# First expert pair fed by a one-hot product, in a two-layer decoder trunk with a mixture of experts

## Chip, cores and metric

The kernel runs on one core of one Trainium2 chip. The metric is the device time of one execution in microseconds (us), as the median of several runs. All times below are of the kernel before the change.

## What is computed

512 tokens of width 1024 pass through two layers. Each layer adds a token mixer and then a mixture of 32 experts. All arithmetic is float32. Cut to what matters here:

```
for i in range(2):
    mk, mv = memory_kv(mem, mem_norm[i], w_mem_kv[i])          # 256 memory tokens
    hn = rms_norm(x, norm_mix[i])
    x  = x + mixer_i(hn, mk, mv) @ w_out[i]                    # layer 0: RG-LRU; layer 1: sparse attention
    h  = rms_norm(x, norm_ffn[i])
    # group of 8 experts (top 1 of 4), then the top 2 experts in that group, for each token
    y  = sum over the token's two experts e of  gate * (silu(h @ w_gate[e]) * (h @ w_up[e])) @ w_down[e]
    x  = x + y
```

## The kernel before

**The experts.** They are worked off in 16 pairs per layer, each pair as one tile of 128 rows: up to 64 tokens of the even expert and up to 64 of the odd one. What goes beyond 64 is left to a loop at the layer's end. A pair needs six weight tiles ("units") of 2 MB each: gate of both experts (j = 0, 1), up (2, 3), down (4, 5). The units go into a ring of 10 places in the arena. SP issues all their loads in order (`weights`, L525 to L536, through `pair_weights`). The first 10 are issued on events of the stage before; each later one waits until TensorE is done with the place's former unit (`gate_psum`, `up_psum`, `y_psum`).

**One pair on TensorE** (`pair`, L1517): gate product (L1480, 32 instructions, written x32), combination of the pair before with x (L1502), up product (L1480), the rest of that combination, transposes of the hidden rows (L1486), then the transposes of the *next* pair's tokens (`tokens_T`, L1473), and the down product (L1494). A float32 product shows two instructions for each matmul in the program. VectorE scales the transposed tokens by norm_ffn into tokT (`tokens_out`, L2063).

**Tokens of a pair.** The normalised rows are stored in DRAM (scratch_xn, L619). GpSimd gathers the 128 rows of a pair with an indirect DMA (`gather`, L723 to L734) into xg; TensorE transposes them. The first pair's gather, transposes and scaling stand before the first pair, the second's inside it, and so on, so there are 17 gathers per layer.

**The handover from mixer to experts.** TensorE follows an order written out by hand: the out products, the transposes of x (fT), router products (route) for four tiles of tokens; then `rank` (how many tokens before this one chose the expert, L1444 to L1452), then `table` (L1456 to L1462), which turns ranks into a table of token numbers for each pair. VectorE picks the experts between route and rank (L1950 to L1984), computes the mixing weights (L1988 to L2001), then the places (L2008 to L2017) and, behind the table, tabP, from which the gathers take their indices. In layer 0, the four memory products of layer 1 (memK.0, memK.1, memV.0, memV.1; L1155) stand between: one before rank, one between rank and table, two behind the table. SP waits for memV.1 before it loads the second pair's up units.

**PSUM banks** are handed out round robin over a list of jobs (`plan`, L148): a job's bank is its number mod 8 and it waits until the job 8 before has been read out by ScalarE or VectorE.

**The start.** ScalarE issues the loads of mem_norm, norm_mix and norm_ffn into `gains` (L792), in runs of 8 numbers; VectorE waits for all three before it spreads the gain over the first transposed tile (L1629, two instructions of 128x512 for each of four tiles of tokens). The first mixer product (xs.0) waits for the eighth of them and for its weights, loaded in two halves (L555).

**Middle of layer 0's mixer.** On TensorE: ..., xs.5, xq.0, xq.1, the six block gates, two norm sums, the transposes of the memory rows (memT, 16), then the memory products, which wait until VectorE has spread two gains over each of four banks (L1629, eight instructions). On VectorE, these stand behind `log_decays(1)` (L1707 to L1716), which waits for the block gates. The first attention logits (x_logits, L1282) wait for the normalised memory keys, the last of VectorE's chain there: two reciprocals of 128x512 (L1623), three scans (L1731), a third reciprocal.

## Time and profile before

| what | us |
|---|---|
| median of 3 runs | 1498.46 (1496.92 to 1500.74) |
| the profiled execution's own time | 1493.24 |
| its span, first to last instruction | 1491.4 |
| TensorE busy | 1385.7 (93%) |
| VectorE busy | 590.6 (40%) |
| ScalarE busy | 326.6 (22%) |
| TensorE's mean granted clock | 0.976 of full |
| main queue (q1, all loads of SP) | 447.96 MB, 72.8% of the 16 DMA engines' time |

The span is one profiled execution; the runs are others of the same program. "Busy" of TensorE counts matmuls up to their modelled ends. A granted clock of 1.00 is 2.4 GHz, 0.50 is 1.2 GHz. Layer 0's experts run from about 266 to 726 us, layer 1's from about 1022 to 1484 us.

### The profile page before, as it was taken

Reading aid. Unit: us, or ns where it says so; the run is one execution under the profiler, and the core shown is the slowest. Engines: PE = TensorE matmul, PEld = TensorE weight load, DVE = VectorE, ACT = ScalarE, POOL = GpSimd, SP = SyncE. Lnnn points to the kernel's source line nnn. Section 1 sums busy time; section 2 is a strip of 40 time slices with the busy share of each in tenths; the row PEclk is TensorE's granted clock in tenths of the full one; section 3 lists DMA queues with packets and bytes.
Section 4 is the critical chain, followed back from the end, with each engine's and each line's share of the span. In section 5 each row is a group of like instructions: output and inputs, shape, how many; then the busy total and the mean of one; then the engine's idle time right before and its main releaser. Section 6 shows DMA issues by size and latency. Waiting matters only on the chain.

```text
span 1491.4 us, 16620 instructions
## 1 busy us (share of the span) xinstructions
PE 1385.7 (93%) x6272; PEld 618.7 (41%) x6337; DVE 590.6 (40%) x1084; ACT 326.6 (22%) x632; POOL 103.0 (7%) x199
## 2 busy tenths in 40 slices
PE   7989998999999999999899978976999999999987
PEld 3445456333333334333454555442333333333333
DVE  5555124133333334233649774132334334332334
ACT  4445111101101101111337664110111111110110
POOL 1001000200000000000000132003000000000000
PEclk9999999999999999999999999987999999999999
DMA  9105365999999999999800020737999999999994
GB/s 315 68 0 198 129 263 203 357 428 426 428 426 425 427 428 428 427 427 419 296 0 1 25 93 1 309 152 275 425 428 427 426 427 426 427 427 427 429 426 203
DMA packets 57332, 457.53 MB, mean 307 GB/s; under 512 B 15516, under 2 KB 22220, under 8 KB 32312
## 3 DMA queue, kind: packets, MB, share of 16 engines
q1 hardware_dynamic: 50928, 447.96, 72.8%
q0 software_dynamic: 5504, 8.68, 1.6%
q8 instruction: 42, 0.69, 0.2%
q10 hardware_dynamic: 840, 0.06, 0.0%
q14 instruction: 18, 0.15, 0.0%
HBM read 459.50 MB, written 10.53 MB: 315 GB/s over the span
## 4 chain that ended last, share of the span: by engine, by line
PE 63%; DMA 23%; DVE 8%; ACT 3%; issue 1%; POOL 0%; SPq 0%; ACTq 0%; DVEq 0%; POOLq 0%
PE ps L1480 20%; PE ps L1155 19%; DMA arena<-in_moe_w_up 14%; PE ps L1494 10%; DMA arena<-in_moe_w_gate 9%; PE ps L1502 6%; PE ps L1473 1%; DVE mix L1774 1%; ACT arena L999 1%; DVE small L1773 1%; DVE arena L1850 1%; DMA mix<-scratch_xn,whole 1%; PE ps L1486 1%; DVE xT L1629 1%; DMA gains<-in_norm_ffn 1%
## 5 line engine op out<-in xcount | busy, mean ns | idle before, releaser
L1480 PE MATMUL ps<-arena,xT 128*64 128x512 f32 x2048 | 461.9, 605 | 26.0 <-DMA arena<-in_moe_w_gate 20.5
L1480 PEld LDWEIGHTS ps<-arena,xT 128*64 128x64 f32 x2048 | 151.6, 139 | 319.2 <-issue 319.2
L2086 DVE TENSOR_TENSOR x<-ps,x 128x1024 f32<-128x1024 f32 x120 | 146.5, 1225 | 219.0 <-PE ps L1502 216.7
L1494 PE MATMUL ps<-arena,xT 128*64 128x512 f32 x1024 | 226.8, 595 | 0.0
L1155 PE MATMUL ps<-xT,arena 128*128 128x512 f32 x384 | 170.6, 599 | 1.8 <-DVE xT L1629 1.4
L1502 PE MATMUL ps<-mix,xT 128*128 128x512 bf16 x660 | 157.4, 379 | 6.4 <-issue 4.8
L1494 PEld LDWEIGHTS ps<-arena,xT 128*64 128x64 f32 x1024 | 70.7, 137 | 131.8 <-issue 127.9
L1155 PE MATMUL ps<-arena,mix 128*128 128x512 f32 (+1 forms) x288 | 119.4, 570 | 0.0
L1502 PEld LDWEIGHTS ps<-mix,xT 128*128 128x128 bf16 x720 | 65.5, 98 | 119.5 <-issue 48.7
L1155 PEld LDWEIGHTS ps<-xT,arena 128*128 128x128 f32 x384 | 72.6, 192 | 92.5 <-issue 89.6
L2069 DVE SCALAR_TENSOR_TENSOR xT<-ps,cur,xT 128x512 f32<-128x512 f32 x32 | 24.0, 751 | 207.3 <-PE ps L1480 207.3
L2079 DVE TENSOR_TENSOR mix<-ps,mix 128x512 f32<-128x512 f32 x60 | 41.5, 692 | 158.4 <-ACT mix L1101 158.4
L1095 ACT ACTIVATE xT<-ps 128x512 f32<-128x512 f32 x32 | 19.1, 597 | 387.1 <-PE ps L1486 387.1
L1101 ACT ACTIVATE mix<-ps 128x512 bf16<-128x512 f32 x60 | 35.8, 597 | 201.9 <-PE ps L1494 201.9
L1155 PEld LDWEIGHTS ps<-arena,mix 128*128 128x128 f32 x288 | 53.8, 190 | 56.7 <-issue 55.8
L728 POOL CAST whole<-tabP 128x1 int32 (+1 forms) x34 | 6.3, 184 | 968.3 <-PE ps L1473 779.7
L1091 ACT ACTIVATE xT<-ps 128x512 f32<-128x512 f32 x32 | 19.1, 597 | 219.0 <-PE ps L1480 219.0
L721 POOL TENSOR_SCALAR arena<-arena,small 128x256 f32<-128x256 f32 (+3 forms) x80 | 39.3, 510 | 248.6 <-DVE small L1789 189.7
L2063 DVE TENSOR_TENSOR xT<-ps,gains 128x512 f32<-128x512 f32 x68 | 43.8, 687 | 22.7 <-PE ps L1473 18.4
L1473 PE MATMUL ps<-ident,mix 128*128 128x128 f32 x272 | 37.0, 280 | 12.9 <-DMA mix<-scratch_xn,whole 12.2
L1936 DVE TENSOR_TENSOR x<-ps,x 128x512 f32<-128x512 f32 x16 | 11.1, 692 | 90.3 <-PE ps L1155 90.3
L2082 DVE TENSOR_TENSOR mix<-mix 128x512 bf16<-128x512 f32 x60 | 41.2, 687 | 2.9
(268 smaller groups left out, 1110.8 us busy)
## 6 DMA issues: line engine op xcount, KB each, us to landing
arena<-in_moe_w_gate SPq DMA_DIRECT2D x64, 2048.0 KB, 32.3
arena<-in_moe_w_up SPq DMA_DIRECT2D x64, 2048.0 KB, 32.0
arena<-in_moe_w_down SPq DMA_DIRECT2D x64, 2048.0 KB, 34.9
arena<-in_w_out SPq DMA_DIRECT2D x2, 4096.0 KB, 13.5
arena<-in_dsa_w_in SPq DMA_DIRECT2D x1, 5120.0 KB, 16.1
arena<-in_w_mem_kv SPq DMA_DIRECT2D x2, 2048.0 KB, 9.0
scratch_xn<-arena SPq DMA_DIRECT2D x8, 512.0 KB, 2.9
scratch_rep<-scratch_bias SPq DMA_DIRECT2D x1, 3840.0 KB, 17.9
```

Source lines behind the costliest of these rows:

```text
L721: ins = pool.tensor_scalar(buf[:, h, 0:width], buf[:, h, 0:width], inv[:, h:h + 1], 1.0, ALU.mult, ALU.mult)
L1101: act.activation(y_hi[part, c, :], ps[part, BANK_Y + c, :], ACT.Copy).then_inc(q["y_high"], 1)
L1155: ins = pe.matmul(b[part, cols], l, r, start=i == 0, stop=i == len(pairs) - 1)
L1473: ins = pe.transpose(ps[:, BANK_XT[k // 4], (k % 4) * P:(k % 4) * P + n], xg[0:n, k::KD][:, 0:P], ident[0:n, 0:n])
L1480: ins = pe.matmul(ps[e * CAP:(e + 1) * CAP, bank, :], tokT[:, k, e * CAP:(e + 1) * CAP], rows_in[u][:, k, :], start=k == 0, stop=k == KD - 1)
L1494: ins = pe.matmul(ps[e * CAP:(e + 1) * CAP, BANK_Y + c, :], hT[:, j, e * CAP:(e + 1) * CAP], rows_down[u][:, j, c * 512:(c + 1) * 512], st ...
L1502: ins = pe.matmul(ps[:, 4 + 2 * (t % 2) + c, :], onehot[part, t * P:(t + 1) * P], y[part, c, :], start=q == 0, stop=q == 2)
L2063: dve.tensor_tensor(tokT[:, 4 * q:4 * q + 4, :], ps[:, BANK_XT[q], :].rearrange("p (k n) -> p k n", k=4), gains[:, 3 * L + 2, 4 * q:4 * q ...
L2069: dve.scalar_tensor_tensor(out=h_sb[part, :], in0=ps[part, BANK_UP, :], scalar=c[part, 1:2], in1=silu[part, :], op0=ALU.mult, op1=ALU.mult ...
L2079: dve.tensor_tensor(y_rest[part, c, :], ps[part, BANK_Y + c, :], y_hi[part, c, :], ALU.subtract).then_inc(q["y_rest"], 1)
L2082: dve.tensor_tensor(y_lo[part, c, :], y_rest[part, c, :], y_mi[part, c, :], ALU.subtract).then_inc(q["y_low"], 1)
L2086: dve.tensor_tensor(x[:, t, :], ps[:, b:b + 2, :].rearrange("p a n -> p (a n)"), x[:, t, :], ALU.add).then_inc(s_, 1)
```

## The change

1. **First pair's tokens.** Gather 0, its transposes and its scaling are gone in both layers. After rank, VectorE makes first_hot, a 0/1 matrix that says which token stands at which place of experts 0 and 1; TensorE multiplies the normalised rows (xn_ffn, still in SBUF) by it: 32 matmuls of 128x128, two banks. The features then stand in blocks of 128 (k·128 + p, not p·8 + k), so the first pair's gate and up weights are loaded in that order, and norm_ffn is needed in that order too: it is loaded into prm_rows by one more DMA, transposed with the parameters and copied over the mem_norm part of gains.
2. **Order of the handover.** Layer 0: all four memory products stand before rank. Both layers: rank, first.0, first.1, table. SP issues the first pair's sixth unit (it lies over xn_ffn) behind first.1. TensorE waits for the old banks behind the first gate product.
3. **Layer 1's units.** The second pair's up units are issued right behind the first five units.
4. **Start.** norm_mix is loaded first and waited for alone; the last half tile is scaled by ScalarE (four instructions of 128x128); xs weights come in three thirds.
5. **Middle of the mixer.** memT is transposed between xq.0 and xq.1; VectorE spreads it before log_decays(1).

```diff
@@ mixer_steps
-             ("xq", 0), ("xq", 1), ("gates", 1), ("sq.xq", 0), ("sq.xq", 1), ("memT", 0), ("mem", 0), ("sq.memK", 0),
+             ("xq", 0), ("memT", 0), ("xq", 1), ("gates", 1), ("sq.xq", 0), ("sq.xq", 1), ("mem", 0), ("sq.memK", 0),
@@ SP
+                if kind < 2 and by_block:
+                    sp.dma_start(rows_in[u], src.rearrange("(k p) n -> p k n", p=P)).then_inc(done, 16)
...
-                weights(L, p * 2 + j % 2, j // 2, u, landed[u])
+                weights(L, p * 2 + j % 2, j // 2, u, landed[u], isinstance(p, int) and p == 0)
...
-                    for h in range(2):
-                        c0 = h * LRU // 2
+                    for h in range(3):
+                        c0 = h * LRU // 3
...
+                    sp.dma_start(prm_rows[R_FFN:NROW, :], a["norm_ffn"].rearrange("l (k p) -> (l k) p", p=P)).then_inc(ld["prm"], 16)
...
                 for j in range(5):
                     pair_weights(L, j, j, 0, NP * L, True)
+                if L:
+                    for j in (2, 3):
+                        pair_weights(L, j, 6 + j, 1, NP * L + 1, True)
...
                 sp.wait_ge(xn_stored, 16 * NT * (L + 1))
-                pair_weights(L, 5, 5, 0, NP * L, True)
                 if L == 0:
                     wait_filled(sp, "1.memV.1")
-                for j in (2, 3):
-                    pair_weights(L, j, 6 + j, 1, NP * L + 1, True)
+                    for j in (2, 3):
+                        pair_weights(L, j, 6 + j, 1, NP * L + 1, True)
+                wait_filled(sp, f"{L}.first.1")
+                pair_weights(L, 5, 5, 0, NP * L, True)
@@ GpSimd
-                gather(L, 0, N, True)
-                gather(L, 1, N + 1)
+                gather(L, 1, N + 1, True)
@@ ScalarE
-            for n, name in enumerate(("mem_norm", "norm_mix", "norm_ffn")):
+            for n, name in ((1, "norm_mix"), (0, "mem_norm"), (2, "norm_ffn")):
...
+                    name = f"0.xT.{NT - 1}.1"
+                    act.wait_ge(ld["gmix"], 16)
+                    wait_filled(act, name)
+                    for k in range(4):
+                        ins = act.activation(xT[:, 4 + k, (NT - 1) * P:S], bank(name)[:, k * P:(k + 1) * P], ACT.Copy,
+                                             scale=gains[:, 1, 4 + k:5 + k])
@@ TensorE
                 if L == 0:
-                    memory_product(1, 0)
+                    for i in range(4):
+                        memory_product(1, i)
                 b = open_bank(f"{L}.rank")
...
+                pe.wait_ge(first_placed, L + 1)
+                for h in range(2):
+                    b = open_bank(f"{L}.first.{h}")
+                    for k in range(4):
+                        for t in range(NT):
+                            ins = pe.matmul(b[:, k * P:(k + 1) * P], xn_ffn[:, t, (4 * h + k) * P:(4 * h + k + 1) * P],
+                                            first_hot[:, t].rearrange("p e n -> p (e n)"), start=t == 0, stop=t == NT - 1)
+                    ins.then_inc(filled, 1)
                 b = open_bank(f"{L}.table")
...
-                    pe.wait_ge(m["xt_sbuf"], n * 2 + (2 * L + 2))
+                    if first:
+                        wait_emptied(pe, f"{L}.first.1")
+                    else:
+                        pe.wait_ge(m["xt_sbuf"], n * 2)
                     both(BANK_GATE, units[0:2], m["gate_psum"])
...
-                pe.wait_ge(gathered, 16 * ((NP + 1) * L + 1))
-                tokens_T(m["xt_psum"])
@@ VectorE
                     x_rows(0)
-                    dve.wait_ge(ld["gains"], 48)
-                    for t in range(1, NT):
+                    x_rows(1)
+                    dve.wait_ge(ld["gmix"], 16)
+                    x_spread(0)
+                    for t in range(2, NT):
...
-                    log_decays(1)
...
+                    line.link(dve.tensor_copy(gains[:, 0:6:3, :], prm[:, R_FFN:NROW].rearrange("p (l k) -> p l k", l=2)))
+                    log_decays(1)
...
                 dve.tensor_tensor(choice[:], oh[0], oh[1], ALU.add).then_inc(chosen, 1)
+                wait_filled(dve, f"{L}.rank")
+                line.link(dve.scalar_tensor_tensor(out=first_row, in0=ranks[:, :, 0:2], scalar=1.0, in1=choice[:, :, 0:2],
+                                                   op0=ALU.add, op1=ALU.mult))
+                dve.tensor_tensor(first_hot, iota_tok[:, 1:CAP + 1].unsqueeze(1).unsqueeze(1).to_broadcast([P, NT, 2, CAP]),
+                                  first_row.unsqueeze(3).to_broadcast([P, NT, 2, CAP]), ALU.is_equal).then_inc(first_placed, 1)
...
                 dve.tensor_copy(dest[:], row).then_inc(routed, 1)
+                for h in range(2):
+                    spread_gain(f"{L}.first.{h}", tokT[:, 4 * h:4 * h + 4, :], 3 * L, h, P)
```

## Rows read from the trace of the kernel before

**Rows 1.** The page, 40 equal slices of 37.3 us: what the DMA engines moved
```profile
GB/s 315 68 0 198 129 263 203 357 428 426 428 426 425 427 428 428 427 427 419 296 0 1 25 93 1 309 152 275 425 428 427 426 427 426 427 427 427 429 426 203
```

**Rows 2.** The chain that ended last, whole program: start, us, what
```profile
309.97 7.02 PE ps L1494 x32
...
337.63 7.02 PE ps L1494 x32
...
651.93 42.62 DMA arena<-in_moe_w_gate
...
1408.25 41.92 DMA arena<-in_moe_w_gate
```

**Rows 3.** Timeline of SP's queue, both handovers: start, us, engine, line, what
```profile
262.43 0.80 SPq L532 DMA_DIRECT2D arena<-in_moe_w_up  x2
272.86 0.80 SPq L535 DMA_DIRECT2D arena<-in_moe_w_down  x2
...
932.57 0.83 SPq L532 DMA_DIRECT2D arena<-in_moe_w_gate  x2
...
1032.13 0.80 SPq L535 DMA_DIRECT2D arena<-in_moe_w_down  x2
```

**Rows 4.** Table of stretches, both handovers: busy us (count) of PE, PEld, DVE, ACT, POOL; PEclk, DMA share, GB/s
```profile
275.00:277.50 2.50, 2.50 (x14) 1.01 (x12) 0.00 (x0) 0.00 (x0) 1.35 (x2) 1.00 1.37 230
...
1025.00:1028.00 3.00, 3.00 (x9) 0.86 (x8) 0.00 (x0) 0.00 (x0) 0.99 (x1) 0.52 0.05 15
1028.00:1032.10 4.10, 4.10 (x22) 1.55 (x20) 0.00 (x0) 0.00 (x0) 2.91 (x4) 1.00 0.02 1
1032.10:1035.00 2.90, 2.90 (x16) 1.01 (x14) 0.00 (x0) 0.60 (x1) 2.29 (x3) 1.00 0.76 91
```

**Rows 5.** Timeline of PE, handover of layer 1: start, us, engine, line, what
```profile
998.40 0.27 PE L1451 MATMUL ps<-choice,ones_b 128*128 128x32 bf16 x4
1002.84 3.65 PE L1460 MATMUL ps<-xT 128*128 128x64 f32 x16 [4.17 <-DVE xT L2020]
1018.71 1.95 PE L1473 MATMUL ps<-ident,mix 128*128 128x128 f32 x8 [12.22 <-DMA mix<-scratch_xn,whole]
1022.19 16.77 PE L1480 MATMUL ps<-arena,xT 128*64 128x512 f32 x64 [1.54 <-DVE xT L2063]
```

**Rows 6.** Timeline of PE, handover of layer 0
```profile
241.16 3.70 PE L1155 MATMUL ps<-arena 128*128 128x256 f32 x16
...
265.74 13.95 PE L1480 MATMUL ps<-arena,xT 128*64 128x512 f32 x64 [1.54 <-DVE xT L2063]
```

**Rows 7.** The chain, layer 1's mixer (64 instructions, 132 columns)
```profile
762.46 7.20 PE ps L1244 x64
```

**Rows 8.** A group of VectorE by form: busy us, mean ns
```profile
L2014 DVE TENSOR_TENSOR xT<-iota_tok,small 128x256 f32<-128x256 f32 x8 | 3.4, 425 | 0.3
```

**Rows 9.** The chain, start of the program
```profile
1.73 8.06 DMA gains<-in_norm_ffn
10.85 1.29 DVE xT L1629 x2
...
17.76 8.71 PE ps L1155 x16
```

**Rows 10.** Timeline of PE, its first transposes
```profile
7.25 1.94 PE L1164 MATMUL ps<-ident,mix 128*128 128x128 f32 x8 [7.25 <-DVE mix L1613]
```

**Rows 11.** Timeline of PE, middle of layer 0's mixer
```profile
102.75 8.86 PE L1155 MATMUL ps<-mix,arena 128*128 128x256 f32 x32 [4.39 <-DVE mix L1629]
111.45 7.07 PE L1155 MATMUL ps<-arena,mix 128*128 128x256 f32 x32
...
126.17 2.00 PE L1282 MATMUL ps<-arena 64*128 64x256 f32 x16
```

**Rows 12.** Timeline of VectorE, the same stretch
```profile
116.92 1.22 DVE L1731 TENSOR_TENSOR_SCAN arena<-arena 128x512 f32<-128x512 f32 x1
120.13 3.35 DVE L1623 RECIPROCAL mix<-mix 128x512 f32<-128x512 f32 x1 [1.99 <-ACT mix L831]
```

More of the change, by code:

```diff
@@ L142, in pt_reader, with x_reader @@
     return "act" if (s + g) % 2 else "dve"
+def x_reader(L, t, h):
+    return "act" if (L, t, h) == (0, NT - 1, 1) else "dve"
 def plan():
@@ L256, in plan @@
             j.add(memory_products(1)[0], "act")
+        if L == 0:
+            for name in memory_products(1)[1:]:
+                j.add(name, "act")
         j.add(f"{L}.rank", "dve")
-        if L == 0:
-            j.add(memory_products(1)[1], "act")
+        for h in range(2):
+            j.add(f"{L}.first.{h}", "dve")
         j.add(f"{L}.table", "dve")
-        if L == 0:
-            for i in (2, 3):
-                j.add(memory_products(1)[i], "act")
     return j
@@ L399, in hybrid_trunk @@
         route_area = flatT[:, 2816:4096]
-        place_hot = flatT[:, 512:1536].rearrange("p (k t c n) -> p k t c n", k=2, t=NT, c=2)
-        expert_pay = flatT[:, 1536:2048].rearrange("p (k t c e) -> p k t c e", k=2, t=NT, c=2)
+        place_hot = flatT[:, 1024:2048].rearrange("p (k t c n) -> p k t c n", k=2, t=NT, c=2)
+        first_hot = flatT[:, 2048:2560].rearrange("p (t e n) -> p t e n", t=NT, e=2)
+        expert_pay = flatM[:, 1024:1536].rearrange("p (k t c e) -> p k t c e", k=2, t=NT, c=2)
+        first_row = small[:, 24:24 + 2 * NT].rearrange("p (t e) -> p t e", t=NT)
         pay_t = small[:, 64:80].rearrange("p (k t c) -> p k t c", k=2, t=NT)
@@ L406, in hybrid_trunk @@
         i8 = route_area[:, 1248:1280].bitcast(U32).rearrange("p (t n) -> p t n", t=NT)
-        ld = {n: sem(f"ld_{n}") for n in ["mem", "x0", "x1", "x2", "x3", "win0", "win1", "prm", "onehot", "gains", "broute", "wkv", "win", "winq", "wing", "wv", "wg",
+        ld = {n: sem(f"ld_{n}") for n in ["mem", "x0", "x1", "x2", "x3", "win0", "win1", "win2", "prm", "onehot", "gmix", "gains", "broute", "wkv", "win", "winq", "wing", "wv", "wg",
                                           "wout", "wr", "bias", "wuv", "ovl"]}
@@ L519, in last_bank @@
             return (jobs.number[f"1.xT.{t}.0"] + c) % 8
-        assert sorted(last_bank(t, c) for t in range(NT) for c in range(2)) == list(range(8)) and last_bank(2, 1) == BANK_Y + 1
+        assert sorted(last_bank(t, c) for t in range(NT) for c in range(2)) == list(range(8))
+        assert all(last_bank(t, c) % 2 == c for t in range(NT) for c in range(2)) and BANK_Y % 2 == 0
         block = ctx.enter_context(nc.Block())
@@ L527, in _, with weights @@
         def _(sp):
-            def weights(L, e, kind, u, done):
-                if kind < 2:
+            def weights(L, e, kind, u, done, by_block=False):
+                if kind < 2 and by_block:
+                    src = a["moe_w_gate" if kind == 0 else "moe_w_up"][L, e]
+                    sp.dma_start(rows_in[u], src.rearrange("(k p) n -> p k n", p=P)).then_inc(done, 16)
+                elif kind < 2:
                     src = a["moe_w_gate" if kind == 0 else "moe_w_up"][L, bass.ds(e, 1)]
@@ L1462, in _, with banks_emptied @@
                 ins.then_inc(filled, 1)
-                if L == 0:
-                    memory_product(1, 2)
-                    memory_product(1, 3)
                 for n in range(state["n"] - 8, state["n"]):
-                    who = jobs.reader[n]
-                    pe.wait_ge(emptied[who], jobs.before[n][who])
+                    if n % 8 == BANK_GATE:
+                        pe.wait_ge(emptied[jobs.reader[n]], jobs.before[n][jobs.reader[n]])
+                def banks_emptied():
+                    for who in ("act", "dve"):
+                        pe.wait_ge(emptied[who], jobs.before[state["n"] - 1][who])
                 def tokens_T(s_, n=P):
@@ L1651, in _ @@
                     rows_normalise(L, "mem", range(2), lambda t: mem[:, t, :], lambda t: mem[:, t, :])
+                    dve.wait_ge(ld["gains"], 32)
                 else:
@@ L2001, in _ @@
                                                 pay_t[:, k].unsqueeze(3).to_broadcast([P, NT, 2, NE]), ALU.mult))
-                wait_filled(dve, f"{L}.rank")
-                ranks = bank(f"{L}.rank")[:, 0:NT * NE].rearrange("p (t e) -> p t e", t=NT)
                 place = [small[:, 16 + NT * k:16 + NT * (k + 1)] for k in range(2)]
```

52 lines of the change are left out of this document (32 added, 20 removed).

## The prediction

> **What bounds the kernel now.** I read the page's slices first. In the middle of either layer's experts the DMA engines move 425 to 429 GB/s [rows 1], one slice like the next. TensorE is busy nearly all the time there too, so the chain of waits has to say who paces whom. It does so late in each layer: the last pair's gate weights are issued at 651.93 and 1408.25 us and land 42.62 and 41.92 us later, at 694.55 and 1450.17, and the chain runs through these landings [rows 2]. Early in a layer it runs through TensorE alone, with a period of 337.63 − 309.97 = 27.66 us a pair [rows 2]. Fifteen periods, 414.9 us, from the first gate product of layer 0 at 265.74 [rows 6] come to 680.6; the weights come at 694.55. So the loads are the bound, by 14 us. In layer 1 the same sum, from 1022.19 [rows 5] with 2.8 us for a gate product of 16.77 instead of 13.95 us [rows 5, 6], gives 1439.9 against 1450.17: 10 us.
>
> What starts that stream of loads? SP's timeline shows it: ten units fit into the ring, and the eleventh is issued at 272.86 in layer 0 and at 1032.13 in layer 1 [rows 3], when the first gate product is done. In layer 1 the DMA engines have nothing to do before that moment (share 0.02 to 0.05) [rows 4]. From that issue to the last gate landing pass 694.55 − 272.86 = 421.7 us and 1450.17 − 1032.13 = 418.0 us. **A microsecond by which the first gate product ends sooner is a microsecond off the layer**, as long as the stretch behind it keeps its length; and whatever TensorE gains in the mixer of layer 0 moves that product. Behind the last landing the work is unchanged.
>
> **Start.** VectorE waits for norm_ffn's landing at 1.73 + 8.06 = 9.79 us, the first two spreads start at 10.85, a tile's scaling later, and xs.0 starts at 17.76 [rows 9]. With norm_mix issued first and alone, the first spreads can follow the first transposes, which end at 7.25 + 1.94 = 9.19 [rows 10]; allowing 0.45 us for the tile scaled in between, that is 1.2 us sooner. VectorE then has the same sequence, one spread of 1.29 / 2 = 0.65 us [rows 9] shorter, since ScalarE takes it. Its transposed bank is there a spread earlier, so its four small copies end about when VectorE does. 1.2 + 0.65 = 1.9 us saved. Bounds: 0.6 (only the spread moves off) and 2.5. The new load of norm_ffn rows adds one issue on SP ahead of mem and of everything behind it, under half a microsecond on a queue whose loads are wanted tens of microseconds later; a smaller first third can't be later than the first half was. Cost nothing; if it is not covered, at most 1 us at the parameters.
>
> **Middle of the mixer.** TensorE idles 4.39 us before the memory products and then takes 8.86 us for 32 instructions whose twins take 7.07 [rows 11]: a half-speed clock after the idle time, 1.8 us. Both go: memT's spreads now lie under xq.1 (7 us against 8 spreads of 0.65 = 5.2). TensorE would win 6.2 us. What is late next is VectorE: its last scan ends at 118.14 and its third reciprocal waits 1.99 us more for ScalarE [rows 12]. Its chain before that doesn't get shorter, because the gates themselves come 1.9 us later (memT stands before them now) while the 5.2 us of spreads leave the path behind them and ScalarE's roots take most of their place. The normalised memory keys then come at 118.14 + 3.35 + 0.65 = about 122.1, instead of 120.13 + 3.35 + 0.65 = 124.1, and x_logits, now behind gate.0 at 126.17 [rows 11], begins then. Saved 4.1 us, with 1.4 us of new idle time. Bounds: 2.0 and 6.2. I take 4.1. The start and this give **6.0 us** on everything in layer 0 behind.
>
> **Handover in layer 0.** Before: 241.16 to 265.74, 24.6 us from the first memory product to the first gate product [rows 6]. After, on TensorE: four memory products at 7.07 for two [rows 11], 14.1; rank with its hand-over 0.5; VectorE's first_row (an estimate of 0.3, hand-over in it) and first_hot. The latter is twice the 128x256 of L2014 at 425 ns [rows 8], less its fixed part: 0.7. Then 32 matmuls of 128x128. The nearest row is layer 1's 64 instructions of 132 columns in 7.20 us [rows 7]: 7.2. The table has 16 instructions, 3.65 us at half clock [rows 5], so 1.9 at full. Two hand-overs, 0.2. Sum 14.1 + 0.5 + 1.0 + 7.2 + 1.9 + 0.2 = 24.9. **0.3 us later, no gain**: gather 0 was hidden under the memory products, which now cover nothing. VectorE's work between rank and table, 4.2 us [rows 5], now stands behind first_hot, under the 7.2 us; if it doesn't, the table waits. Bounds: 1 sooner and 2.5 later.
>
> Behind the first gate product the queue is emptier than it was: up units of the second pair went out at 262.43 [rows 3] and were still under way at 272.86, with a gather and the eight scatters (a stretch at 230 GB/s with a share of 1.37 [rows 4] shows what scatters do). Now they go out about 7 us sooner relative to TensorE. The difference of 421.7 and 418.0 is what that costs; I give back half: **−1.8 us**, bounds 0 and −3.7.
>
> **Handover in layer 1.** Before: rank is done at 998.40 + 0.27 = 998.7, table 1002.84, 12.22 us of waiting for the gather, transposes 1018.71, scaling, then gate and up product together from 1022.19 [rows 5], the gate half's event at 1032.1 [rows 3]. After: first_hot done at 999.8. TensorE has had little to do for some microseconds, so it starts at half clock. How long? Before, work began at 1022.19, the clock still stood at 0.52 until 1028 and at 1.00 after it [rows 4]: 5.6 us. The first 5.6 us of the product do 25 instructions at 0.225 us, the other 39 take 4.4: done at 1009.8. Table 1.9, gate from 1011.7, first half until 1018.7 at full clock. 1032.1 − 1018.7 = 13.4 us sooner. The scatters, which before fell mostly on an idle queue (91 GB/s at the end of them [rows 4]), now fall on the stream: +1.2. **Layer 1 gains 12.2 us.** Bounds: all at half clock, 64 at 0.225 = 14.4, table 3.65, half a cold gate product, gives 1.1 + 14.4 + 3.7 + 7 + 2.8 behind 998.7, that is 1027.7: a gain of 4.4, less 1.2. All at full clock: 15.
>
> A rule bears on this. The rows show an idle TensorE at half clock and a return some microseconds into the work. The Trainium skill, "TensorE: Matmul & The Clock Gate", Part 1, says that the point of the return varies between runs of the same kernel. By it, the 1.1 us hole before first.0 in layer 0 may or may not cost a half-speed spell; priced by the 8.86 against 7.07 us [rows 11], the sum would be 1.8 us more with one.
>
> The block-ordered weights of the first pair come in runs of 2 KB instead of 16. They are issued from 932.57 [rows 3], 75 us before they are wanted at about 1010; I cost them at nothing. Layer 1's second up units, moved ahead, are 2 of 10 units loaded before the stream anyway and no longer press on the gap; nothing waited for them. The 17th gather was 0.5 MB in each layer outside the stream: nothing.
>
> **Sum**, against the profiled execution: 1493.24 − 6.0 + 0.3 − 1.8 − 12.2 = 1473.5. The median of the runs lies 5.2 us above that execution (1498.46), so I forecast **1479 us** (1478.7). A measurement of this kernel can tell some 0.3%, 4.5 us, from no change.
>
> **Rivals.**
> - *Cold product* (0.12). The clock stays at half through first.0 and first.1 in layer 1 and falls in layer 0's hole as well. For it: the clock was still at 0.52 up to 1028 [rows 4], with a table and transposes done in between. Against: neither of those was a long piece of work. Gain 3.2 in layer 1 instead of 12.2, 1.8 lost in layer 0: 1478.7 + 9.0 + 1.8 = 1489.5.
> - *VectorE holds the mixer, or the stream doesn't follow* (0.12). The mixer gives only its lower bounds (2.6 instead of 6.0) and the stretch of 418 to 422 us grows by 2 because scatters, gather and loads meet: 1484.
> - *The change does nothing that counts* (0.03): the first gate product is not what releases the stream, but a later event such as the first down product, itself unmoved. Against: the eleventh unit goes out 7.12 us behind the start of the gate product in layer 0, 272.86 against 265.74 [rows 3, 6], which is one gate product. 1494 to 1499.
> - *Slower: the block-ordered units arrive late* (0.02). Four units, 8.4 MB, in 2 KB runs, between 932.57 [rows 3] and first.1 at about 1010. They decide only if they take longer than 77 − 15 = 62 us, that is below 135 GB/s, and to turn 20 us of gain into a loss of 5 they would need 87 us, 96 GB/s. None of the full slices goes so low [rows 1]. That would be 1504. The Trainium skill, "DMA: Bandwidth & Descriptors", "Why small descriptors are slow", has a fixed overhead per packet that speaks against shorter runs; by its figures (3 cycles on 64) the four units would take 1 us more, an estimate, and all of it would be hidden.
>
> The forecast itself has 0.71. **Range**: its own terms run from 1473 (mixer 8.7, stretch −3.7, layer 1 at 14) to 1486; the low end with some run-to-run spread 1472, the high end takes in most of the cold product, 1489. Faster by over 0.3%: 0.94 (all but the last two and a few unlucky sums); within 0.3%: 0.04; slower: 0.02.
>
> **What would show it.** xs.0 near 15.9; x_logits 0 some 6 us sooner than 126.17; first gate product of layer 0 near 260.0, so layer 0's eleventh unit near 267; last gate landing near 687; between rank and the first gate product of layer 1 13 us instead of 23.5, with no wait on a gather; the clock at 1.00 in that gate product. A wait of TensorE on VectorE before the table, or on a unit of the first pair, would prove me wrong, as would an eleventh unit that goes out sooner without the last landing following it.

## The result, and the profile after

| | before | after |
|---|---|---|
| median, us | 1498.24 (4 runs, 1496.92 to 1500.74) | 1473.82 (4 runs, 1472.13 to 1474.37) |
| profiled execution, us | 1493.24 | 1473.94 |
| its span, mean granted clock | 1491.4, 0.976 | 1472.0, 0.986 |

The ratio is 0.9833, with a 95% interval of 0.9816 to 0.985: 24.4 us faster by the medians, 19.3 by the two profiled executions. The forecast was 1479, and 19.7 us between the profiles. One execution of experiment 10 took 3039.51 us, about twice as long as all others, for a reason that no trace shows; it is left out of that experiment's median.

The page of the changed kernel, the 40 slices of what the DMA engines moved:

```profile
GB/s 292 96 0 226 139 247 195 385 427 426 427 427 427 426 427 428 427 427 427 321 2 1 1 119 2 310 199 297 427 427 425 427 427 426 427 427 428 428 426 199
```

The plateau is as high as before [rows 1]; it only starts sooner. The start and the middle of the mixer, on TensorE (start, us, engine, line, what, and in brackets the idle time before it):

```profile
15.49 7.10 PE L1181 MATMUL ps<-xT,arena 128*128 128x512 f32 x16 [1.34 <-DVE xT L1668]
...
94.05 7.07 PE L1181 MATMUL ps<-mix,arena 128*128 128x256 f32 x32
...
117.76 2.67 PE L1309 MATMUL ps<-arena 64*128 64x256 f32 x16 [2.00 <-DVE arena L1663]
120.36 8.11 PE L1181 MATMUL ps<-xT,arena 128*128 128x512 f32 x16
```

xs.0 starts 2.3 us sooner than in [rows 9] and takes 7.10 instead of 8.71 us. The 4.39 us before the memory products [rows 11] are gone. The logits start 8.4 us sooner and now wait 2.00 us for VectorE; behind that wait they and the next gate product take 2.67 and 8.11 us where 2.00 [rows 11] and 7.13, as the later gate products of this profile, are usual: in this profile part of the gain is paid back in clock (a "spell" below is such a stretch at a granted clock of one half). The first out product starts at 166.6 instead of 173.4.

The two handovers on TensorE; first layer 0's:

```profile
230.64 1.16 PE L1190 MATMUL ps<-ident,x 128*128 128x128 f32 x8 [0.78 <-DVE x L1983]
232.62 1.95 PE L1181 MATMUL ps<-w_route,xT 128*128 128x36 f32 x16 [0.83 <-ACT xT L1099]
234.40 15.75 PE L1181 MATMUL ps<-arena 128*128 128x256 f32 x64
...
251.52 7.38 PE L1488 MATMUL ps<-xT,arena 128*128 128x128 f32 x64 [1.03 <-issue]
258.74 1.90 PE L1495 MATMUL ps<-mix,xT 128*128 128x64 f32 x16
```

then layer 1's, where [rows 5] had a wait of 12.22 us and a first gate and up product that began at half clock (16.77 us, now 13.96):

```profile
992.18 0.18 PE L1476 MATMUL ps<-choice,before 128*128 128x32 bf16 x1 [4.80 <-DVE choice L2031]
...
993.75 10.16 PE L1488 MATMUL ps<-xT,arena 128*128 128x128 f32 x64 [1.03 <-issue]
1003.75 1.90 PE L1495 MATMUL ps<-mix,xT 128*128 128x64 f32 x16
1005.57 13.96 PE L1516 MATMUL ps<-arena,xT 128*64 128x512 f32 x64
```

The stream behind them. SP's queue issues the eleventh unit at

```profile
267.69 0.82 SPq L548 DMA_DIRECT2D arena<-in_moe_w_down  x2
...
1012.70 0.80 SPq L548 DMA_DIRECT2D arena<-in_moe_w_down  x2
```

and the last gate weights come, by layer 0's timeline of TensorE and by layer 1's chain of waits, at

```profile
687.52 7.09 PE L1516 MATMUL ps<-arena,xT 128*64 128x512 f32 x32 [1.51 <-DMA arena<-in_moe_w_gate]
```

```profile
1390.60 40.15 DMA arena<-in_moe_w_gate
```

From the issue to this: 419.8 us in layer 0 (about 419.6 to the landing itself), and 1390.60 + 40.15 − 1012.70 = 418.05 us in layer 1, against 421.7 and 418.0 from issue to landing before. Both layers still end behind a landing of gate weights; all of the gain but the 2 us of layer 0's stretch lies ahead of the stream.

### The profile page after: what moved, and what is told of

Its sections match the earlier page's. It is cut to its first block and busy times, and to the rows that moved or that the text cites. A ratio compares the mean times of both kernels' runs of the same rounds, so it can differ in the third digit from the quotient of the medians.

```text
span 1472.0 us, 16830 instructions
## 1 busy us (share of the span) xinstructions
PE 1389.9 (94%) x6384; PEld 628.3 (43%) x6449; DVE 592.4 (40%) x1088; ACT 326.9 (22%) x636; POOL 101.0 (7%) x195
## 5 line engine op out<-in xcount | busy, mean ns | idle before, releaser
L1130 ACT ACTIVATE mix<-mix 128x512 bf16<-128x512 f32 x60 | 37.6, 627 | 7.2 <-DVE mix L2133 7.2
```

Source lines behind the costliest of these rows:

```text
L1130: act.activation(y_mi[part, c, :], y_rest[part, c, :], ACT.Copy).then_inc(q["y_mid"], 1)
```

## Experiments

Twelve experiments, in three groups; each group shares its chip and its runs of the kernel before, whose medians were 1497.09 (18 runs), 1496.73 (17) and 1497.77 (11). The theory under test is the prediction's: TensorE's own path to the first gate product sets the stream's start, and the stream then has a fixed length. The changed kernel itself ran only beside the result's four runs of before, so its 1473.82 comes from another group than the medians set against it. Three experiments that moved nothing measurable (6, 8 and 11, one in each group) came to 1473.42, 1473.47 and 1473.34, which supports that comparison; the ratio to each group's own runs of before is given as well.

**1. The kernel before, once more** (label before_again, no edit).

> The kernel before, once more, with a profile. The change moved the median by 24.4 us and the profiled execution by 19.3 (1493.24 to 1473.94). Theory: the mechanisms give 19.3, and the other 5 are the spread of the kernel before, whose runs lie 1493 to 1501. Then its profile shows, in some stretch (a clock or a landing), what is longer in an ordinary run than in the one first profiled. Rival: the first profile was of an ordinary run and another chip gives 1498 with the same stretches all a little longer.

Measured 1497.23 (10 runs, 1495.54 to 1499.38), ratio 1.0009 (0.9998 to 1.0019). Its profiled execution, 1497.96 us, is 4.7 longer than the one that the prediction rests on. Its TensorE shows where:

```profile
242.36 6.06 PE L1155 MATMUL ps<-arena 128*128 128x256 f32 x16
...
255.34 1.97 PE L1460 MATMUL ps<-xT 128*128 128x64 f32 x16 [3.03 <-DVE xT L2020]
...
269.39 13.96 PE L1480 MATMUL ps<-arena,xT 128*64 128x512 f32 x64 [1.54 <-DVE xT L2063]
...
744.79 9.11 PE L1203 MATMUL ps<-xT,arena 128*64 128x512 f32 x32
```

The first memory product takes 3.70 us in [rows 6] and 6.06 here. The handover of layer 0 (first memory product to first gate product) takes 27.0 us here, 24.6 in [rows 6], and 26.7 and 27.6 in experiments 2 and 3, which have it unchanged; layer 1's first projection 9.11 us, against 7.09 in the first profile and 8.81 and 9.24 in 2 and 3. The first profile was the lucky one in both places.

**2. The new start alone, on the kernel before** (start_only).

```diff
-            for n, name in enumerate(("mem_norm", "norm_mix", "norm_ffn")):
+            for n, name in ((1, "norm_mix"), (0, "mem_norm"), (2, "norm_ffn")):
...
-                    dve.wait_ge(ld["gains"], 48)
+                    dve.wait_ge(ld["gmix"], 16)
```

> The kernel before with the new start alone (norm_mix first, last half tile on ScalarE, xs weights in thirds). Theory: xs.0 at 15.5 instead of 17.8, and at full clock, 7.1 instead of 8.7 us; together 2.3 to 3.9 us sooner at the second product. Later in the mixer the memory products wait for VectorE, which also starts sooner, so all of it reaches x_logits and the end: 1493.2 to 1495 against 1497.1. Rival (the middle waits for VectorE's gates, which do not move with the start): under 1 us.

Measured 1494.44 (12 runs), ratio 0.9979 (0.9968 to 0.999): 2.3 us by medians, 3.1 by the ratio. xs.0 starts at 15.4 but takes 8.80 us, so the clock's part did not come in this profile. The lead of the start is kept up to the router:

```profile
171.13 20.87 PE L1168 MATMUL ps<-arena,mix 128*128 128x512 f32 x48
...
237.11 3.19 PE L1168 MATMUL ps<-w_route,xT 128*128 128x36 f32 x16 [0.83 <-ACT xT L1086]
```

The first out product starts 2.3 us sooner than in the first profile and 2.5 sooner than in experiment 1 (173.41 and 173.63), router product 3 also 2.3 and 2.5 sooner (239.39 and 239.60). The first gate product, at 266.80, is 2.6 us sooner than in experiment 1, but 1.1 later than in the first profile with its short handover.

**3. New start and new middle, on the kernel before** (mixer_only).

```diff
-             ("xq", 0), ("xq", 1), ("gates", 1), ("sq.xq", 0), ("sq.xq", 1), ("memT", 0), ("mem", 0), ("sq.memK", 0),
+             ("xq", 0), ("memT", 0), ("xq", 1), ("gates", 1), ("sq.xq", 0), ("sq.xq", 1), ("mem", 0), ("sq.memK", 0),
```

> The kernel before with only the new start and the new middle of layer 0's mixer. Theory: all of layer 0 behind it moves by 6.8 us, as the two profiles show at the first out product, the eleventh unit's issue and the last gate landing follow one for one, layer 1 follows: 6 to 8 us below the kernel before. Rival (the loads would have come when they come anyway): less than 2 us.

Measured 1488.39 (9 runs), ratio 0.9945 (0.9932 to 0.9958): 8.7 us. The mixer's part of the change is about a third of the whole. Less experiment 2, it gives the middle 6.4 us by the medians and 5.1 by the ratios. The profiles of 2 and 3, both with 8.80 us for xs.0, say 4.3: the first out product starts at 166.85 instead of 171.13. The logits wait as in the changed kernel, but no spell follows:

```profile
119.61 2.00 PE L1296 MATMUL ps<-arena 64*128 64x256 f32 x16 [2.00 <-DVE arena L1638]
121.54 7.13 PE L1168 MATMUL ps<-xT,arena 128*128 128x512 f32 x16
```

**4. The changed kernel with its old middle** (middle_undone). The order of the steps goes back too.

```diff
+                    log_decays(1)
                     for mt in range(2):
...
                     line.link(dve.tensor_copy(gains[:, 0:6:3, :], prm[:, R_FFN:NROW].rearrange("p (l k) -> p l k", l=2)))
-                    log_decays(1)
```

> The changed kernel with the middle of layer 0's mixer as it was: memT transposed behind the norm sums, VectorE's log_decays(1) ahead of its spreads. Theory (the middle gained 4.1 us by the prediction, about 4.5 by the landmarks of the before-and-after traces, and all of it reaches the end): 1477.5 to 1478.5 us, the 4.4 us wait before the memory products back, first attention logits 4 to 5 us later than 117.8. Rival (the gain of the middle came from the start, by banks and clock, and the move itself is worth little): 1475 or less.

Measured 1476.35 (4 runs, 1474.99 to 1478.44), ratio 0.9865: 2.5 us slower than the changed kernel by medians, 4.8 by the two ratios, whose groups of before runs differ by 1.5 us. By the medians the theory's size fell short, and the rival's 1475 was passed. The logits are 4.3 us late, as expected, but the first out product only 2.7 (169.35 against 166.64), because the changed kernel's profile has a spell behind the logits and this one has none. That spell is not the rule: of the eight profiles with the 2.00 us wait, only the changed kernel's and experiment 5's have it. Against experiment 6, whose mixer is the changed kernel's and whose profile has neither this spell nor one in xs.0, the middle is worth 4.3 us again, as between 2 and 3. First out products of this experiment and of 6:

```profile
169.35 20.87 PE L1181 MATMUL ps<-arena,mix 128*128 128x512 f32 x48
```

```profile
165.01 20.87 PE L1178 MATMUL ps<-arena,mix 128*128 128x512 f32 x48
```

This profile also shows the four memory products without a spell, behind the same two holes (idle times of 0.79 and 0.83 us) that the changed kernel has:

```profile
237.11 14.06 PE L1181 MATMUL ps<-arena 128*128 128x256 f32 x64
```

**5. The one-hot product done twice** (first_twice).

```diff
+                        for t in range(NT):
+                            pe.matmul(b[:, k * P:(k + 1) * P], xn_ffn[:, t, (4 * h + k) * P:(4 * h + k + 1) * P],
+                                      first_hot[:, t].rearrange("p e n -> p (e n)"), start=t == 0, stop=t == NT - 1)
+                    for k in range(4):
```

> The changed kernel with the one-hot product done twice in both layers (same result, 64 instructions more in each). Theory: 7.0 us more before the first gate product in each layer, and the whole stream of loads moves by that: 14 us slower than the changed kernel. Rival: the loads pace the layer and TensorE has 10 to 14 us in hand in each, so the extra product vanishes in it: 0 to 3 us.

Measured 1487.40 (4 runs), ratio 0.9941 (0.9919 to 0.9962): 13.6 us slower than the changed kernel by medians, 15.0 by the profiled executions, 16 by the two ratios. The added halves on TensorE in layer 0, and the end of the stream in layer 1's chain:

```profile
251.90 3.81 PE L1488 MATMUL ps<-xT,arena 128*128 128x128 f32 x32 [1.03 <-issue]
...
262.69 3.74 PE L1492 MATMUL ps<-xT,arena 128*128 128x128 f32 x32
```

```profile
1404.31 41.65 DMA arena<-in_moe_w_gate
```

Its eleventh unit of layer 1 goes out at 1027.96 and the last gate weights land 418.0 us later, at 1445.96. The product and its copy take 14.36 us in layer 0 (266.26 − 251.90, the table's start) against 7.22, and 16.15 against 10.00 in layer 1, where the cold part is a little shorter: 13.3 us more on TensorE. In the profiles the eleventh unit of layer 1 goes out 15.3 us later and the last weights land 15.2 later, so the stream follows its event one for one; the 2 us beyond the added work gathered on the way (0.4 by the first out product, 1 in layer 0's stretch, the rest in layer 1's mixer). The rival's 0 to 3 us is out: what is added ahead of the stream comes out in full, in both layers.

**6. Layer 1's up units not moved ahead** (up_not_early).

```diff
-                if L:
-                    for j in (2, 3):
-                        pair_weights(L, j, 6 + j, 1, NP * L + 1, True)
```

> The changed kernel with layer 1's units in the old order (second pair's up units behind the stores of the rows). Theory: they then load in the time between the last store and the first gate product in which the queue has nothing to do, and nothing waits for them: 0 us, within 1 of the changed kernel. Rival (the new order is worth something): the sixth unit or the first gather lands so late behind them that the first down product or the second pair's tokens wait: 2 to 5 us more.

Measured 1473.42 (4 runs), ratio 0.985 (0.9828 to 0.9871): nothing that these runs can tell, as argued. In its profile layer 1's eleventh unit goes out 1.3 us sooner than the changed kernel's (1011.43), by luck of the clock in layer 0, and the last weights land only 0.2 sooner (1430.57): a stretch of 419.1 us, where the changed kernel and experiments 5, 7, 9, 10, 11 and 12 have 417.1 to 418.4. So that part of the change may be worth about 1 us; one profile doesn't show it.

**7. The first pair's weights in long runs** (long_runs).

```diff
-                weights(L, p * 2 + j % 2, j // 2, u, landed[u], isinstance(p, int) and p == 0)
+                weights(L, p * 2 + j % 2, j // 2, u, landed[u], False)
```

> The changed kernel with the first pair's gate and up weights of both layers loaded in the old order of rows (16 KB in one piece for each partition instead of eight of 2 KB). The features no longer match the weights of that pair, so its part of the output is of mixed-up features; the work is otherwise the same. Theory (the pieces of 2 KB cost issue time on SP and nothing on the path, because these units are wanted 75 us later): time within 0.5 us of the changed kernel; issue of two such units on SP falls from 10 us to 1 us or less. Rival (the small pieces hold the stream or other loads beside them): 1 us or more less.

This kernel leaves out the matching order of features and weights, so its output is not the program's. Measured 1475.38 (4 runs, 1472.82 to 1475.88), ratio 0.9855 (0.9834 to 0.9875): not faster. The median is 1.6 us above the changed kernel's where 0.5 was allowed for, and the two sets of runs overlap; in the profiles the last weights land 1.0 us sooner. SP's queue with block order and with long runs, first pair of layer 1:

```profile
927.02 10.32 SPq L542 DMA_DIRECT2D arena<-in_moe_w_up  x2
```

```profile
927.08 1.12 SPq L545 DMA_DIRECT2D arena<-in_moe_w_up  x2
```

and what the DMA engines did (stretch, busy us and count of PE, PEld, DVE, ACT, POOL, granted clock, DMA share, GB/s), again the changed kernel first:

```profile
930.00:945.00 15.00, 15.00 (x42) 7.16 (x41) 2.99 (x5) 3.21 (x5) 0.00 (x0) 1.00 1.04 386
```

```profile
930.00:945.00 15.00, 15.00 (x43) 7.11 (x42) 2.99 (x5) 3.21 (x5) 0.00 (x0) 1.00 1.00 428
```

Runs of 2 KB cost 10% of the rate in this stretch and hold SP's queue for 5 us a unit, both long before anyone waits.

**8. Rank between the memory products** (rank_second): layer 0's memV.0 and memV.1 stand behind rank.

```diff
-                    for i in range(4):
+                    for i in range(2):
                         memory_product(1, i)
...
+                    for i in range(2, 4):
+                        memory_product(1, i)
```

> The changed kernel with one order undone in part: in layer 0, rank stands between memK.1 and memV.0 instead of behind memV.1. Theory (the stream follows the first gate product 1:1, and what TensorE waits for VectorE's first_row and first_hot is on that path): memV.0 and memV.1 cover the 1.03 us wait before first.0, and the half-clock spell that the trace of the changed kernel shows in this handover has one hole less to begin in. First gate product of layer 0 1.0 to 1.5 us sooner after rank's own place is allowed for (26.2 us from the first memory product becomes about 25), last landing of layer 0 the same amount sooner, time 1.0 to 1.5 us less. Rival (the half-clock spell comes anyway, or another wait takes the hole's place, such as ScalarE's emptying of the banks): within 0.5 us of the changed kernel.

Measured 1473.47 (5 runs), ratio 0.984 (0.9823 to 0.9858): no gain. The wait before the one-hot product is gone, but the handover is as long as it was, 26.1 us:

```profile
235.01 9.97 PE L1182 MATMUL ps<-arena 128*128 128x256 f32 x32
...
245.18 7.15 PE L1182 MATMUL ps<-arena 128*128 128x256 f32 x32
252.17 7.31 PE L1492 MATMUL ps<-xT,arena 128*128 128x128 f32 x64
```

The rival held: 9.97 us for 32 instructions that take 7.07 at full clock. The hole before the one-hot product is gone and the spell came all the same, ahead of it; that leaves the two holes before the memory products as its suspects.

**9. Memory products in the two holes before them** (holes_filled). The order of the last tile in layer 0 becomes out, memK.0, fT.3, memK.1, route.3, memV.0, memV.1, rank.

```diff
+    if L == 0:
+        order = out_order()
+        order.insert(order.index(("fT", 3)), ("mem", 0))
+        order.insert(order.index(("route", 3)), ("mem", 1))
+        return order
```

> The changed kernel with two of layer 0's four memory products moved forward into the two holes of the last tile: memK.0 before the transposes fT.3, memK.1 before route.3; memV.0 and memV.1 stay before rank. Theory (TensorE's own path sets layer 0's first gate product, and the half-clock spell in the memory products follows the two short holes of 0.78 and 0.83 us before it): both holes gone, 1.6 us, and with them the spell of 1.65 us; first gate product of layer 0 at 257.3 to 259 instead of 260.6, time 1.6 to 3.3 us less. Rival 1 (the spell comes elsewhere, as it did in the run with rank second): 0 to 1 us less. Rival 2 (the choice of experts, which now starts 5.5 us later on VectorE, ends behind the memory products): rank waits, nothing gained or a loss.

Measured 1471.04 (5 runs), ratio 0.9819 (0.9802 to 0.9836): 2.8 us less than the changed kernel by medians, 2.1 by the ratios, whose intervals overlap, and 2.3 less than experiment 11 of the same group.

```profile
229.66 3.62 PE L1188 MATMUL ps<-arena 128*128 128x256 f32 x16
233.12 1.04 PE L1197 MATMUL ps<-ident,x 128*128 128x128 f32 x8
234.00 3.62 PE L1188 MATMUL ps<-arena 128*128 128x256 f32 x16
237.45 1.87 PE L1188 MATMUL ps<-w_route,xT 128*128 128x36 f32 x16
239.16 7.15 PE L1188 MATMUL ps<-arena 128*128 128x256 f32 x32
...
256.73 5.80 PE L1525 MATMUL ps<-arena,xT 128*64 128x512 f32 x26
```

No hole, no spell; the first gate product starts 3.8 us sooner (256.73 against 260.57) from the same first out product at 166.6. VectorE's choice of experts stayed under the memory products: rank waits for nothing. How much of the 3.8 us is the edit's stays open: 1.6 us are the holes, but the spell was missing in experiment 4's profile too, with the holes there. Nor did all of it arrive: the last gate product of layer 0 starts 2.0 us sooner (685.56), 421.7 us behind the eleventh unit's issue instead of 419.8, and the profiled execution is 1.4 us shorter.

**10. A gate product before the logits** (gate_ahead).

```diff
-             ("gate", 0), ("x_logits", 0), ("x_logits", 1), ("gate", 1), ("x_turn", 0), ("x_logits", 2),
+             ("gate", 0), ("gate", 1), ("x_logits", 0), ("x_logits", 1), ("gate", 2), ("x_turn", 0), ("x_logits", 2),
```

> The changed kernel with gate.1 of layer 0's mixer ahead of the first attention logits, and each later gate one place earlier. Theory (the 2.00 us in which the logits wait for VectorE's chain, and the half-clock spell behind it, 0.67 + 1.0 us, are the middle's unfinished gain): first out product 2.0 to 3.7 us sooner, time 2 to 3.7 us less. Rival (the wait comes back at the end of the mixer, where the last turn now has one gate product less to cover ScalarE's and VectorE's softmax): less than 1 us.

Measured 1471.24 (5 runs, 1467.99 to 1473.85), ratio 0.9822 (0.9803 to 0.9841): 2.6 us less by medians, 1.6 by the ratios, whose intervals overlap. The wait is gone. The first out product starts at 162.83, 3.8 us sooner than in the changed kernel's profile, but 2.2 sooner than in experiment 6's, which has the wait and no spell: the edit is worth the wait. The first gate product is 2.2 us sooner than the changed kernel's (258.41), since the memory products now take 16.7 us, with a longer spell.

**11. Work for an idle TensorE** (keep_warm): five matmuls between route.3 and rank in layer 1, which rank overwrites.

```diff
+                if L:
+                    pe.wait_ge(rows_normed, rows[L, "ffn", NT - 2])
+                    for i in range(5):
+                        pe.matmul(b[:, 0:256], xn_ffn[:, 0, 0:P], xn_ffn[:, 1, 0:256], start=True, stop=True)
```

> The changed kernel with five matmuls of 128x256 between route.3 and rank in layer 1, while TensorE waits 4.8 us for the choice of experts; what they compute is overwritten by rank and read by nobody. Theory (the one-hot product of layer 1 takes 10.16 us instead of 7.3 because TensorE stood idle before it): 7.3 to 8.5 us for it, time 1.5 to 3 us less. Rival 1 (the two holes that are left, about 0.4 before rank and 1.0 behind it, keep the clock at half all the same): 10.2 us, no change. Rival 2 (at half clock the five take 4.4 us and end behind the choice): up to 0.5 us more.

Measured 1473.34 (5 runs), ratio 0.9832 (0.9812 to 0.9851): nothing to be told from the changed kernel. The table of stretches, the product, and the same product in experiments 7 and 9, without the five matmuls:

```profile
987.00:990.00 3.00, 2.68 (x14) 2.07 (x13) 2.38 (x17) 0.73 (x2) 0.00 (x0) 1.00 0.85 262
990.00:992.00 2.00, 0.00 (x0) 0.00 (x0) 1.86 (x15) 0.80 (x2) 0.00 (x0) 0.96 0.82 319
992.00:994.00 2.00, 0.82 (x15) 0.75 (x16) 1.25 (x6) 0.69 (x1) 0.00 (x0) 0.50 0.98 418
994.00:998.00 4.00, 4.00 (x20) 4.00 (x20) 3.69 (x15) 0.00 (x0) 0.00 (x0) 0.50 1.01 434
```

```profile
993.73 9.74 PE L1492 MATMUL ps<-xT,arena 128*128 128x128 f32 x64 [1.03 <-issue]
```

```profile
993.61 8.89 PE L1488 MATMUL ps<-xT,arena 128*128 128x128 f32 x64 [1.03 <-issue]
```

```profile
992.66 10.33 PE L1497 MATMUL ps<-xT,arena 128*128 128x128 f32 x64 [1.03 <-issue]
```

At full clock the five took 2.40 us and ended at 989.7; TensorE then stood idle until rank, the granted clock fell from 1.00 to 0.50 meanwhile, and the product took 9.74 us. That is no gain: without the five it takes 10.16 us in the changed kernel and 8.89 to 10.33 in experiments 4, 6, 7, 8, 9 and 10. Rival 1 held, with a gap before rank of 2.4 us rather than 0.4, since the five ran at full clock.

**12. Experiments 9, 10 and 11 together** (all_three).

> The changed kernel with all three edits: memory products in the holes, gate.1 ahead of the logits, five matmuls before rank in layer 1. Theory: the three lie one behind another on the path and add, 1473.6 less 5 to 10 = 1464 to 1469 us, faster than both kernels. Rival (half-clock spells removed in one place come back in another, as the run with rank second and the undone middle hint): the sum of the three single gains falls short by 2 us or more.

Measured 1466.51 (5 runs, 1466.26 to 1469.12), ratio 0.9799 (0.9782 to 0.9815): 7.3 us less than the changed kernel by medians, 5.1 by the ratios, where the single gains sum to 5.8 and 3.9. The theory's 1464 to 1469 us held and the sum did not fall short. It is the fastest of all the kernels here, and its interval lies clear of the changed kernel's. Here the five matmuls ran at half clock (4.09 us) and left a gap of 0.78 us before rank; the one-hot product took 9.01 us, within the spread above. Its eleventh unit of layer 1 goes out at 1005.52 and its last gate weights land at

```profile
1383.38 40.05 DMA arena<-in_moe_w_gate
```

which is 1423.43, again 417.9 us later.

## Why the prediction was right, point by point

- **The bound and the 1:1 rule** held. The event, that is the issue of the eleventh unit, moved by 5.2 us in layer 0 (272.86 to 267.69) and 19.4 in layer 1 (1032.13 to 1012.70), the last landings by 7.3 (of which 2 are a shorter stretch) and 19.4, the end by 19.3. Experiments 5 and 12 moved the event in both directions with stretches of 418.0 and 417.9. That is layer 1, where all but two profiles (4 and 8, whose chains don't pass that landing) show 417.1 to 419.1. In layer 0 the stretch is less fixed, as the point on the emptier queue says.
- **Start**: 1.9 us taken, 2.3 in the profile (1.8 against experiment 1, where xs.0 starts at 17.30), 2.3 to 3.1 in experiment 2. In the changed kernel's profile 1.6 us of half clock in xs.0 went too; it stays in those of experiments 2, 3, 8, 9, 11 and 12, so it isn't bound to the edit.
- **Middle**: 4.1 taken. VectorE came out late next, as said, with a wait of 2.00 us instead of the estimated 1.4, and the logits started 8.4 us sooner where 6.0 was forecast. Of the 8.4, 1.6 are the clock in xs.0, and a spell of the same size behind the new wait took as much away again. With start and middle together the first out product came 6.8 us sooner, against 6.0. Where neither spell differs between the profiles, the middle gave 4.3 us on the old kernel (2 against 3) and on the new one (4 against 6): the 4.1 was right in size and mechanism.
- **Handover in layer 0**: 24.9 us expected, 26.2 came (260.57 − 234.40). The one-hot product took 7.38, taken as 7.2, the table 1.90, and VectorE's part between rank and table lay under the product. The miss is the memory products, 15.75 us for an estimated 14.1. The prediction tied a spell to the 1.1 us hole before first.0 (1.03 in the trace), with no price in the sum and 1.8 us beside it; the page that it names there speaks of the clock's return and not of whether a hole costs a spell. A spell came with 1.65 us, but ahead of that hole. Experiments 8 and 9 fit with the holes before the products as its place, but experiment 4 has these holes and no spell, so what decides stays open. The forecast of "no gain" rests on the first profile's 24.6 us, too: against the 26.7 to 27.6 of the other three profiles of the old handover, the changed one is 0.5 to 1.4 us shorter.
- **Emptier queue**: the stretch of layer 0 shrank from 421.7 to about 419.6 (the landing 0.2 us before the product's start, as before); 1.8 us taken, 2 came. It was a guess of half a difference, and no experiment isolates its cause. To the start of the last gate product, the four profiles of the old handover show 421.6 to 422.0 us, those of the new one 419.6 to 420.9, but experiment 9's 421.7.
- **Handover in layer 1**: 13.4 us from rank to the event. The event moved by 19.4 and the first instruction of rank by 6.0 (998.13 to 992.18), so 13.5 came; 2.8 of it is that the first half of the gate product now takes 7.13 us instead of 9.94. The product took 10.16 us against a forecast of 10.0 that let 5.6 us of half clock run at its head. The table of stretches of the changed kernel shows that:

```profile
992.00:994.00 2.00, 0.78 (x15) 0.74 (x16) 1.18 (x6) 0.64 (x1) 0.00 (x0) 0.50 0.94 401
994.00:996.00 2.00, 2.00 (x10) 2.00 (x11) 1.86 (x9) 0.00 (x0) 0.00 (x0) 0.50 1.09 467
996.00:998.00 2.00, 2.00 (x12) 2.00 (x11) 1.83 (x7) 0.00 (x0) 0.00 (x0) 0.50 0.99 426
998.00:1000.00 2.00, 2.00 (x13) 2.00 (x13) 0.78 (x5) 0.00 (x0) 0.00 (x0) 0.61 0.50 201
1000.00:1002.00 2.00, 2.00 (x21) 2.00 (x20) 0.69 (x1) 0.00 (x0) 0.00 (x0) 1.00 0.02 8
```

  The 1.2 us taken off for scatters on the stream did not show: the stretch is 418.05 against 418.0.
- **What the sum had at nothing, and luck**: the 7.3 us at layer 0's last landing had shrunk to 6.0 at layer 1's rank. The sum let them pass whole; layer 1's first projection took 8.77 us where the first profile had 7.09. This 1.3 us and the scatters' 1.2, which never came, cancel, and 0.8 us more from start and middle make up for part of the 1.3 more that layer 0's handover took. That the sum for the profiles came within 0.4 us is in part luck; its large terms, 6.0 and 13.4, were close (6.8 and 13.5).
- **Costed at nothing**: the 2 KB runs, the early up units. Experiment 7 agrees, and experiment 6 to within about 1 us. The Trainium skill, "DMA: Bandwidth & Descriptors", "Why small descriptors are slow", puts a fixed overhead on each packet; by its figures the prediction had 1 us for four units. The trace agrees in direction and shows about twice the size: the rate fell from 428 to 386 GB/s, some 2 us on 8.4 MB, hidden all the same.
- **The median: the step that failed.** The sum for the profile was 0.4 us off, the median 5 us. The prediction added to its sum the 5.2 us by which the median of before lay above its profiled execution, as if a constant. It was a property of that one execution: experiment 1 shows that its handover of layer 0 was 2.4 us shorter and layer 1's first projection 2 us faster than in another execution of the same program, and experiments 2 and 3 have the longer ones. The changed kernel's profiled execution lies at its own median (1473.94 and 1473.82). Against the profile of experiment 1 the gain is 24.0 us, against the median's 24.4. The measured 1473.8 is still inside the stated range, 2 us above its lower end. Of the rivals none came: the one-hot product ran at half clock for about its first 5.7 us and at full clock after, the stream followed, nothing in the first pair was waited for.

## What to carry to other kernels

When a stream of loads has a fixed length, look for the event that releases it and cost every edit by how far it moves that event; what lies behind it need not be touched. Tokens that are still in SBUF can be selected by a one-hot product on an idle TensorE instead of a round trip through DRAM: 10.2 us in place of a 12.2 us wait, transposes and scaling. Short waits of TensorE can cost more than they show, because a half-clock spell may follow; moving independent matmuls into them took the waits away (experiment 9), and the spell with them in the two profiles that there are. Before trusting one profiled execution to a few microseconds, take a second one or set it against the median; before blaming a spell on an edit, look whether the same place has it in kernels without the edit.

## What the runs showed of the chip

- **A granted clock of one half comes in spells behind holes of under one to a few microseconds, and wanders between executions.** The same 16 instructions took 3.70 and 6.06 us in two executions of one program; a spell cost 1.6 to 2.9 us. Its place is not set by the kernel alone: behind the same 2.00 us wait it is there in two profiles and missing in six, in xs.0 of the kernels with the new start there in six and missing in six, and the memory products behind the same two holes took 14.06 to 16.71 us (experiments 4 and 10). With these holes filled (9 and 12) it was missing in both profiles. The Trainium skill, "TensorE: Matmul & The Clock Gate", Part 1, says that the point of return varies between runs; the 3.70 and 6.06 us fit with that, but don't tell a later return from a fall that came in one execution only. That this explains the whole spread of before, 1492.6 to 1501.8 us over 46 runs, is argued from one pair of profiles, not shown (the 46 are those of the three groups).
- **Filling the first half of an idle time gave nothing that can be told.** With TensorE busy for the first half of a 4.8 us wait the granted clock still fell to 0.50 before its end, and the next product's 9.74 us lie within the 8.89 to 10.33 that it takes without the filling (experiment 11).
- **A load in 2 KB runs holds SP's queue for 5.2 us per 2 MB**, against 0.6 in long runs, and the stretch with such loads moved 386 GB/s against 428.
